# Experts of layers 0 and 1: 96 rows as three thirds in four column tiles

## The chip, the core and the metric

The kernel runs on one core of a Trainium2 chip, as one program. The metric is its device time in microseconds: 3403.63 us is the median of three runs of the kernel before (3401.73 to 3408.33). Everything is fp32. Five engines matter: TensorE (PE) multiplies, with its weight loads shown apart as PEld; VectorE (DVE), ScalarE (ACT) and GpSimd (POOL) work on tiles; SyncE (SP) issues most transfers, which 16 DMA engines carry out. ACT and POOL issue transfers too, each on a queue of its own: SP's is q1, ACT's q10, POOL's q0.

## The reference

The whole computes two transformer layers on 512 tokens of width 1024, then a third block. The part at hand is the mixture of experts at the end of each of the first two layers:

```
scores = sigmoid(x @ router_w)                      # 512 tokens x 16 experts
idx    = the two best experts of the best group;  w = their scores, made to sum to 1
rows of x are sorted by expert and padded to blocks
hb = silu(xb @ w_gate[e]) * (xb @ w_up[e])          # 1024 -> 512, twice
y  = hb @ w_down[e]                                 # 512 -> 1024
out[token] += y[row] * w
```

Each expert has three matrices of 2 MB: gate and up [1024, 512], down [512, 1024].

## The kernel before, in words

A layer's experts run in two stages, each behind a barrier of all engines: `route`, then `moe_experts`.

**Routing.** DVE works out for each token its two slots among blocks of 96 rows and, for each block, its expert (`blk_e`). POOL scatters the rows of `x` to a DRAM buffer `slots` by indirect DMA. Block 0 does not take this way: DVE builds a one-hot matrix `oneh` [token, 96], and PE multiplies (L1206) with `x` as the stationary side (128 columns of it at a time) and `oneh` as the moving side (96 columns), which gives block 0 with its features on partitions; ACT copies it from PSUM to `xg0` (L1214).

**Experts.** The trace holds 16 blocks a layer, handled in 8 pairs, each pair with two sets of buffers, r = 0 and 1. The loop's body on PE (L1468 on) is: gate and up of r = 0, of r = 1, then down of r = 0, of r = 1. A block of 96 rows is cut in a main part of 64 rows and a tail of 32:

- `gate_up` (L1436): the stationary side is 64 columns of `xg`, so the array is two column tiles of 64; gate's product goes to PSUM partitions 0 to 63, up's to 64 to 127, 512 columns each.
- `gate_up_tail` (L1446): 32 columns of `xg`, four column tiles of 32, each with 256 moving columns: two quarters for gate, two for up.
- `down` (L1458, L1464): the same cut, 64 rows in two tiles of 512 columns, 32 rows in four tiles of 256.

ACT takes a sigmoid of gate and copies up to partitions 0 to 63 (L1539, L1540, L1544, L1545), since DVE multiplies partition by partition; DVE multiplies twice (L1503, L1505, L1512, L1514) and turns the hidden rows for `down` in 32x32 blocks, one instruction for each 32 partitions (L1509 eight times, L1517 four). ACT copies the results out (L1551, L1552), and POOL stores them in six transfers a block (L1585, L1587); SP does so for the last two blocks (L1420, L1422).

**What sets the order.** Each engine runs its own loop; semaphores tie them. SP (`load_pair`) reloads a set's gate and up when the set's last gate/up matmul is done (`tail_ready`), and its down when its last down matmul is done (`down_ready`); the six loads of a pair stand in one queue in the order gate0, up0, gate1, up1, down0, down1. ACT loads the 96 rows of a coming block from `slots` (L1556, one transfer of 96 partitions by 4 KB), and DVE turns them into `xg` with twelve instructions (`turn_x`, L1497). On DVE the order is `gated(i, 0)`, `turn_x` of the next pair's r = 0, `gated(i, 1)`, `turn_x` of r = 1. `w_ready`, `xg_ready`, `hT_main`, `hT_tail` and `y_copied` are what PE waits for.

Around it: `ExpertWeights` loads four (layer 0) or five (layer 1) of the first six matrices in the stage before and the rest during `route`; `expert_sum` gathers the results after it.

Of the kernel before, what the change touches and what calls it, by code (L numbers as in the profile page):

```python
# [51 lines left out]
MOE_ROWS, MOE_BLOCKS = 96, 26  # L52
SLOT_ROWS = -(-MOE_ROWS * MOE_BLOCKS // 128) * 128
# [1104 lines left out]
def route(nc, name, x, escore, router_b, sbr, idx, strict, ones, iota, mo, xg0, slots_dram, put):  # L1158
# [5 lines left out]
    with stage(nc, name) as st:  # L1164
# [6 lines left out]
        cm, first_ps = st.ps("cm"), [st.ps(f"first{h}") for h in range(2)]  # L1171
# [16 lines left out]
        with nc.Block() as block:  # L1188
# [6 lines left out]
            @block.tensor  # L1195
            def _(pe):
                pe.wait_ge(m_ready, 1)
                nc.tensor.matmul(cm[:, 0:NT * E], strict[:], flat(both[:]), start=True, stop=False)
                nc.tensor.matmul(cm[:, 0:NT * E], ones[:], flat(acc[:, 0:NT, :]), start=False, stop=True)
                nc.tensor.matmul(cm[:, NT * E:(NT + 1) * E], ones[:], acc[:, NT, :], start=True, stop=True).then_inc(cum_ready, 1)  # L1200
                pe.wait_ge(oneh_ready, 1)
                for h in range(2):
                    for c in range(4):
                        for t in range(NT):
                            k = 4 * h + c
                            mm = nc.tensor.matmul(first_ps[h][:, c * MOE_ROWS:(c + 1) * MOE_ROWS], x[:, t, k * P:(k + 1) * P],  # L1206
                                                  oneh[:, t, :], start=(t == 0), stop=(t == NT - 1))
                    mm.then_inc(first_ready, 1)

            @block.scalar  # L1210
            def _(act):
                for h in range(2):
                    act.wait_ge(first_ready, h + 1)
                    nc.scalar.activation(xg0[:, 4 * h:4 * h + 4, :].rearrange("p c s -> p (c s)"),  # L1214
                                         first_ps[h][:, 0:4 * MOE_ROWS], ACT.Copy)
# [11 lines left out]
            def _(dve):  # L1227
# [126 lines left out]
                V.tensor_scalar(blk_e[:, B:B + 1], nbl[:], float(E // 2 - 1), None, ALU.add)  # L1354

def moe_load(sp, w, w_ready, weights, n, e, near=True):

    rows = weights[n][ds(e, 1)]
    src = rows.rearrange("a (p j) n -> p (a j) n", p=P) if near else rows.rearrange("a (k p) n -> p (a k) n", p=P)  # L1360
    sp.dma_start(w[n][:], src).then_inc(w_ready[n], 16)

def moe_experts(nc, name, sbr, xg0, slots_dram, weights, y_dram, w, w_ready, put):
# [4 lines left out]

    blk_e = sbr[4]  # L1370
    KF = D_EXP // P
    MB, MAIN, TAIL = MOE_ROWS, 64, 32
    QD = 32
    lo, hi = slice(0, MAIN), slice(MAIN, P)
    last = MOE_BLOCKS // 2 - 1
    with stage(nc, name) as st:
        xs = [st.sb(f"xs{r}", [MB, D]) for r in range(2)]
        xs_ready = [st.sem(f"xs_ready{r}") for r in range(2)]
        xg = [xg0, st.sb("xg1", [P, KD, MB])]
        sig, up, hid = ([st.sb(f"{n}{r}", [MAIN, D_EXP]) for r in range(2)] for n in ("sig", "up", "hid"))  # L1380
        tsig, tup, thid = ([st.sb(f"{n}{r}", [MAIN, D_EXP // 2]) for r in range(2)] for n in ("tsig", "tup", "thid"))
        hT = [st.sb(f"hT{r}", [P, KF, MB]) for r in range(2)]
        yb = [st.sb(f"y{r}", [P, 512]) for r in range(2)]
        ytb = [st.sb(f"yt{r}", [P, 256]) for r in range(2)]
        gu_ps = [st.ps(f"gu_ps{r}") for r in range(2)]
        tgu_ps = [st.ps(f"tgu_ps{r}", (P, 256)) for r in range(2)]
        y_ps, ty_ps = [st.ps(f"y_ps{r}") for r in range(2)], [st.ps(f"ty_ps{r}", (P, 256)) for r in range(2)]
        xg_ready = st.sem("xg_ready")
        main_ready, tail_ready = st.sem("main_ready"), st.sem("tail_ready")
        act_main, act_tail = st.sem("act_main"), st.sem("act_tail")  # L1390
        hid_main, hid_tail = st.sem("hid_main"), st.sem("hid_tail")
        hT_main, hT_tail = st.sem("hT_main"), st.sem("hT_tail")
# [6 lines left out]
        with nc.Block() as block:  # L1399

            @block.sync
            def _(sp):
                def load_pair(i):

                    e = [sp.value_load(blk_e[0:1, ds(2 * i + 2 + r, 1)], min_val=0, max_val=N_EXP - 1) for r in range(2)]
                    for r in range(2):
                        sp.wait_ge(tail_ready, 2 * i + r + 3)
                        moe_load(sp, w[r], w_ready[r], weights, 0, e[r])
                        moe_load(sp, w[r], w_ready[r], weights, 1, e[r])
                    for r in range(2):  # L1410
                        sp.wait_ge(down_ready, 2 * i + r + 3)
# [4 lines left out]
                for r in range(2):  # L1416
                    b = 2 * n1 + r
                    sp.wait_ge(y_copied, b + 3)
                    for h, part in enumerate((lo, hi)):
                        sp.dma_start(y_dram[ds(b * MB, MAIN), h * 512:(h + 1) * 512], yb[r][part, :]).then_inc(last_out, 16)  # L1420
                    for q in range(4):
                        sp.dma_start(y_dram[ds(b * MB + MAIN, TAIL), q * 256:(q + 1) * 256],  # L1422
                                     ytb[r][q * TAIL:(q + 1) * TAIL, :]).then_inc(last_out, 16)
                sp.wait_ge(last_out, 16 * 12)

            @block.tensor
            def _(pe):
                def gate_up(i, r):
                    b = 2 * i + r
                    pe.wait_ge(xg_ready, b + 1)  # L1430
                    for n in range(2):
                        pe.wait_ge(w_ready[r][n], 16 * i + 16)
                    pe.wait_ge(hid_main, b + 1)
                    for k in range(KD):
                        for n, part in enumerate((lo, hi)):
                            mm = nc.tensor.matmul(gu_ps[r][part, :], xg[r][:, k, 0:MAIN],  # L1436
                                                  w[r][n][:, k * D_EXP:(k + 1) * D_EXP], start=(k == 0), stop=(k == KD - 1))
                    mm.then_inc(main_ready, 1)

                def gate_up_tail(i, r):  # L1440
                    b = 2 * i + r
                    pe.wait_ge(hid_tail, b + 1)
                    for k in range(KD):
                        for q in range(4):
                            n, c0 = q // 2, k * D_EXP + q % 2 * 256
                            mm = nc.tensor.matmul(tgu_ps[r][q * TAIL:(q + 1) * TAIL, :], xg[r][:, k, MAIN:MB],  # L1446
                                                  w[r][n][:, c0:c0 + 256], start=(k == 0), stop=(k == KD - 1))
                    mm.then_inc(tail_ready, 1)

                def down(i, r):  # L1450
                    b = 2 * i + r
                    pe.wait_ge(hT_main, b + 1)
                    pe.wait_ge(w_ready[r][2], 16 * i + 16)
                    pe.wait_ge(y_copied, b + 1)
                    for f in range(KF):
                        for h, part in enumerate((lo, hi)):
                            c0 = f * D + h * 512
                            nc.tensor.matmul(y_ps[r][part, :], hT[r][:, f, 0:MAIN], w[r][2][:, c0:c0 + 512],  # L1458
                                             start=(f == 0), stop=(f == KF - 1))
                    pe.wait_ge(hT_tail, b + 1)  # L1460
                    for f in range(KF):
                        for q in range(4):
                            c0 = f * D + q * 256
                            mm = nc.tensor.matmul(ty_ps[r][q * TAIL:(q + 1) * TAIL, :], hT[r][:, f, MAIN:MB],  # L1464
                                                  w[r][2][:, c0:c0 + 256], start=(f == 0), stop=(f == KF - 1))
                    mm.then_inc(down_ready, 1)
# [2279 lines left out]
```

## Time and profile before

| | us |
|---|---|
| runs of the kernel before | 3401.73, 3403.63, 3408.33 |
| span of the profiled execution | 3408.2 |
| expert stage of layer 0 (first matmul to the next stage's first work) | 405.3 to 689.8 |
| expert stage of layer 1 | 1101.7 to 1385.2 |
| PE busy, DVE busy, ACT busy | 3050.8, 1764.9, 633.8 |

The page gives no time of the profiled execution apart from its span; the span is 4.6 us above the median of the runs and 0.1 us below the slowest. The two expert stages take 568 us of it, a sixth. In the page's 40 slices (85 us each) they are slices 5 to 8 and 13 to 16. A busy share is no measure of a bound: in these stages PE and the DMA engines are both busy nearly all the time, and only the waits and the landing times tell them apart. A matmul of fp32 is two instructions in the trace, each with its own weight load.

### The profile page before, as it was taken

Reading aid. Unit: us, or ns where it says so; the run is one execution under the profiler, and the core shown is the slowest. Engines: PE = TensorE matmul, PEld = TensorE weight load, DVE = VectorE, ACT = ScalarE, POOL = GpSimd, SP = SyncE. Lnnn points to the kernel's source line nnn. Section 1 sums busy time; section 2 is a strip of 40 time slices with the busy share of each in tenths; the row PEclk is TensorE's granted clock in tenths of the full one; section 3 lists DMA queues with packets and bytes.
Section 4 is the critical chain, followed back from the end, with each engine's and each line's share of the span. In section 5 each row is a group of like instructions: output and inputs, shape, how many; then the busy total and the mean of one; then the engine's idle time right before and its main releaser. Section 6 shows DMA issues by size and latency. Waiting matters only on the chain. (4 is left out here: it accounts for less than half of the span.)

```text
span 3408.2 us, 40873 instructions
## 1 busy us (share of the span) xinstructions
PE 3050.8 (90%) x15195; PEld 1424.4 (42%) x15195; DVE 1764.9 (52%) x3808; ACT 633.8 (19%) x1348; POOL 348.5 (10%) x439
## 2 busy tenths in 40 slices
PE   7888799989987999799999999898699988898887
PEld 5445433334554333454444444665432332333232
DVE  6523488732343888339999910564333242424334
ACT  1134112122321111200100110453110100101011
POOL 0113111110222111010000000123100000000000
PEclk9989799989987999799999999999799999999998
DMA  7965399840042999343335245863399999999996
GB/s 263 251 216 218 133 396 394 349 132 31 13 173 96 349 400 404 133 160 120 110 121 149 97 162 175 300 215 152 158 384 428 429 428 429 428 429 429 428 428 291
DMA packets 188225, 886.19 MB, mean 260 GB/s; under 512 B 32120, under 2 KB 71936, under 8 KB 151760
## 3 DMA queue, kind: packets, MB, share of 16 engines
q1 hardware_dynamic: 156464, 794.98, 59.4%
q0 software_dynamic: 28288, 77.91, 6.5%
q10 hardware_dynamic: 3360, 11.80, 1.1%
q8 instruction: 71, 1.16, 0.1%
q14 instruction: 42, 0.34, 0.0%
HBM read 803.59 MB, written 80.99 MB: 260 GB/s over the span
## 5 line engine op out<-in xcount | busy, mean ns | idle before, releaser
L3384 PE MATMUL ec_gu<-ec_ring,ec_xg 128*64 128x512 f32 x2032 | 484.2, 622 | 92.7 <-DVE xT L3465 56.7
L245 PE MATMUL proj_ps<-xT,proj_w 128*128 128x512 f32 x992 | 430.7, 596 | 0.0
L245 PE MATMUL proj_ps<-proj_w,xT 128*128 128x512 f32 (+2 forms) x896 | 358.3, 562 | 6.6 <-DMA proj_w<-in_w_in 4.1
L3384 PEld LDWEIGHTS ec_gu<-ec_ring,ec_xg 128*64 128x64 f32 x2032 | 151.9, 143 | 412.6 <-issue 317.9
L245 PEld LDWEIGHTS proj_ps<-xT,proj_w 128*128 128x128 f32 x992 | 189.4, 191 | 237.5 <-issue 237.0
L245 PEld LDWEIGHTS proj_ps<-proj_w,xT 128*128 128x128 f32 x896 | 171.3, 192 | 191.6 <-issue 157.3
L1497 DVE STREAM_TRANSPOSE moe_xg<-moe_xs 32x256 f32<-32x256 f32 x360 | 229.1, 637 | 38.9 <-DMA moe_xs<-slots 33.5
L1436 PE MATMUL moe_gu_ps<-moe_w,moe_xg 128*64 128x512 f32 x1024 | 231.8, 606 | 10.7 <-DVEq L1486 4.8
L3404 PE MATMUL ec_yp<-ec_ring,ec_hT 128*64 128x512 f32 x1024 | 225.8, 597 | 9.5 <-issue 6.6
L274 ACT ACTIVATE proj_o<-proj_ps 128x512 f32<-128x512 f32 (+1 forms) x120 | 70.9, 590 | 611.6 <-PE proj_ps L245 611.6
L3545 ACT ACTIVATE xT<-ec_gu 64x512 f32<-64x512 f32 x64 | 37.8, 591 | 757.3 <-PE ec_gu L3384 756.1
L2546 DVE SCALAR_TENSOR_TENSOR band_big<-proj_hit,proj_row,band_big 128x516 f32<-128x516 f32 x256 | 173.5, 749 | 2.4
L2546 DVE SCALAR_TENSOR_TENSOR band_acc<-proj_hit,proj_row,band_acc 128x512 f32<-128x512 f32 x256 | 172.5, 746 | 2.4
L3478 DVE STREAM_TRANSPOSE ec_hT<-xT 32x256 f32<-32x256 f32 x256 | 160.9, 628 | 5.5
L3465 DVE TENSOR_TENSOR xT<-xT,ec_gu 64x512 f32<-64x512 f32 x64 | 41.6, 676 | 225.4 <-ACT xT L3546 224.9
L3459 DVE TENSOR_TENSOR x<-x,ec_x 128x512 f32<-128x512 f32 x58 | 39.9, 688 | 224.5 <-PE ec_x L3364 224.4
L1458 PE MATMUL moe_y_ps<-moe_w,moe_hT 128*64 128x512 f32 x512 | 120.3, 613 | 27.2 <-DVE moe_hT L1509 27.2
L1436 PEld LDWEIGHTS moe_gu_ps<-moe_w,moe_xg 128*64 128x64 f32 x1024 | 73.2, 139 | 153.8 <-issue 153.8
L3404 PEld LDWEIGHTS ec_yp<-ec_ring,ec_hT 128*64 128x64 f32 x1024 | 72.2, 138 | 156.1 <-issue 147.0
L1446 PE MATMUL moe_tgu_ps<-moe_w,moe_xg 128*32 128x256 f32 x2048 | 117.1, 380 | 0.0
L722 PE MATMUL mix_o<-out_w,xT 128*128 128x512 f32 x256 | 112.7, 600 | 3.2 <-PEq L89 3.2
L1509 DVE STREAM_TRANSPOSE moe_hT<-moe_hid 32x128 f32<-32x128 f32 x256 | 103.1, 403 | 6.0
(527 smaller groups left out, 3626.4 us busy)
## 6 DMA issues: line engine op xcount, KB each, us to landing
ec_ring<-in_w_up SPq DMA_DIRECT2D x64, 2048.0 KB
ec_ring<-in_w_down SPq DMA_DIRECT2D x64, 2048.0 KB
ec_ring<-in_w_gate SPq DMA_DIRECT2D x63, 2048.0 KB
moe_w<-in_exp_w_gate SPq DMA_DIRECT2D x32, 2048.0 KB, 13.0
moe_w<-in_exp_w_up SPq DMA_DIRECT2D x32, 2048.0 KB, 17.0
moe_w<-in_exp_w_down SPq DMA_DIRECT2D x32, 2048.0 KB, 19.9
proj_w<-in_w_in SPq DMA_DIRECT2D x22, 2048.0 KB, 10.9
proj_w<-in_w_ada SPq DMA_DIRECT2D x16, 1536.0 KB
```

The lines of the kernel that those rows point to most:

```text
L245: mm = nc.tensor.matmul(bank[0:jb["op"], 0:jb["ow"]], lhs, rhs, start=(k == 0), stop=(k == nk - 1))
L274: e = nc.scalar.activation(row, bank, jb["func"], scale=jb["scale"])
L722: mm = nc.tensor.matmul(o_ps[t % 2][q][:], xT[:, k, t * P:(t + 1) * P], w[q][:, k, :], start=(k == 0), stop=(k == KD - 1))
L1436: mm = nc.tensor.matmul(gu_ps[r][part, :], xg[r][:, k, 0:MAIN], w[r][n][:, k * D_EXP:(k + 1) * D_EXP], start=(k == 0), stop=(k == KD - 1))
L1446: mm = nc.tensor.matmul(tgu_ps[r][q * TAIL:(q + 1) * TAIL, :], xg[r][:, k, MAIN:MB], w[r][n][:, c0:c0 + 256], start=(k == 0), stop=(k == K ...
L1458: nc.tensor.matmul(y_ps[r][part, :], hT[r][:, f, 0:MAIN], w[r][2][:, c0:c0 + 512], start=(f == 0), stop=(f == KF - 1))
L1497: e = V.transpose(xg[r][fq, :, tb], near(xs[r][tb, :], KD)[:, :, fq])
L1509: e = V.transpose(hT[r][fq, :, tb], near(hid[r][tb, :], KF)[:, :, fq])
L2546: V.scalar_tensor_tensor(acc[:, h, 0:wd], self.hit[r][:, 0:wd], self.row[r][:, h:h + 1], acc[:, h, 0:wd], ALU.mult, ALU.add)
L3384: mm = nc.tensor.matmul(gu_ps[n][half, :], xg[:, k, c0:c0 + CAP], w[m][:, j * D_FF + n * 512:j * D_FF + (n + 1) * 512], start=(k == 0), st ...
L3404: mm = nc.tensor.matmul(y_ps[half, :], hT[:, f * CAP:(f + 1) * CAP], w[:, j * D + hh * 512:j * D + (hh + 1) * 512], start=(f == 0), stop=( ...
L3478: e = V.transpose(cols.rearrange("p (d j s) -> p d j s", j=4, s=CAP)[:, :, :, tb * QD:(tb + 1) * QD], rows.rearrange("p (d q j) -> p d j q ...
```

## The change

All 96 rows are handled alike, as three thirds of 32 rows, each in four column tiles:

- `gate_up`: a third's four tiles have 256 moving columns each, 128 of gate and the same 128 of up side by side. For this gate and up lie in one SBUF tensor `[P, 2, KD * D_EXP]`. A product's gate and up columns then stand on the same partitions, so ACT makes one sigmoid of a third and DVE reads up straight from PSUM.
- `down`: a third's four tiles have 256 columns each.
- `turn_x` and the turning of the hidden rows are one instruction of 128 partitions for a third. For this `xs` holds quarter c of the features on partitions 32c to 32c+31, and its load is four transfers of 32 partitions by three runs of 1 KB.
- PSUM has three banks for gate/up and three for down, one for each third, which both sets use.
- Results are stored in four transfers a block instead of six, 32 partitions by three runs of 1 KB.
- Routing: `oneh` is the stationary side (32 columns) and `x` the moving side (256 columns); ACT copies three thirds to `first_sb`, and DVE turns them.
- All expert matrices have the near layout (a partition's rows adjacent in DRAM, 16 KB); gate and up of set 0 had the other before, in their first load. The early loads are gate0, up0, gate1, up1 (and down0 in layer 1).

```diff
@@ route
-                for h in range(2):
-                    for c in range(4):
-                        for t in range(NT):
-                            k = 4 * h + c
-                            mm = nc.tensor.matmul(first_ps[h][:, c * MOE_ROWS:(c + 1) * MOE_ROWS], x[:, t, k * P:(k + 1) * P],
-                                                  oneh[:, t, :], start=(t == 0), stop=(t == NT - 1))
+                for th in range(THIRDS):
+                    for t in range(NT):
+                        for c in range(4):
+                            mm = nc.tensor.matmul(first_ps[th][QD * c:QD * c + QD, :], oneh[:, t, th * QD:(th + 1) * QD],
+                                                  x[:, t, c * 256:(c + 1) * 256], start=(t == 0), stop=(t == NT - 1))
                     mm.then_inc(first_ready, 1)
...
+                for th in range(THIRDS):
+                    dve.wait_ge(first_copied, th + 1)
+                    V.transpose(xg0[:, th], first_sb[:, th, :].rearrange("p (q j) -> p j q", j=KD))
@@ moe_experts
+    rows_of = lambda dram, b, c: dram[ds(b * MB, MB), c * 256:(c + 1) * 256].rearrange("(t p) n -> p t n", p=QD)
...
+                    for th in range(TH):
+                        pe.wait_ge(xg_ready, TH * b + th + 1)
+                        pe.wait_ge(hid_done, TH * b + th + 1)
+                        for k in range(KD):
+                            for c, part in enumerate(quarter):
+                                c0 = k * D_EXP + c * P
+                                mm = nc.tensor.matmul(gu_ps[th][part, :], xg[r][:, th, k, :], w[r][0][:, :, c0:c0 + P],
+                                                      start=(k == 0), stop=(k == KD - 1))
+                        mm.then_inc(gu_ready, 1)
...
+                    for th in range(TH):
+                        pe.wait_ge(hT_ready, TH * b + th + 1)
+                        pe.wait_ge(y_copied, TH * b + th + 1)
+                        for f in range(KF):
+                            for c, part in enumerate(quarter):
+                                c0 = f * D + c * 256
+                                mm = nc.tensor.matmul(y_ps[th][part, :], hT[r][:, th, f, :], w[r][1][:, c0:c0 + 256],
+                                                      start=(f == 0), stop=(f == KF - 1))
+                        mm.then_inc(down_ready, 1)
...
-                    for fq in quads:
-                        for tb in quads[:MB // QD]:
-                            e = V.transpose(xg[r][fq, :, tb], near(xs[r][tb, :], KD)[:, :, fq])
+                    for th in range(TH):
+                        V.transpose(xg[r][:, th], near(xs[r][:, th, :], KD)).then_inc(xg_ready, 1)
...
+                    for th in range(TH):
+                        dve.wait_ge(act_done, TH * b + th + 1)
+                        V.tensor_mul(sig[r][:, th, :], sig[r][:, th, :], gu_ps[th][:, 0:P])
+                        V.drain()
+                        V.tensor_mul(hid[r][:, th, :], sig[r][:, th, :], gu_ps[th][:, P:2 * P]).then_inc(hid_done, 1)
+                        V.drain()
+                        V.transpose(hT[r][:, th], near(hid[r][:, th, :], KF)).then_inc(hT_ready, 1)
...
-                    act.dma_start(xs[r][:], slots_dram[ds(b * MB, MB), :]).then_inc(xs_ready[r], 16)
+                    for c, part in enumerate(quarter):
+                        act.dma_start(xs[r][part], rows_of(slots_dram, b, c)).then_inc(xs_ready[r], 16)
...
-                    for h, part in enumerate((lo, hi)):
-                        pool.dma_start(y_dram[ds(b * MB, MAIN), h * 512:(h + 1) * 512], yb[r][part, :]).then_inc(stored, 16)
-                    for q in range(4):
-                        pool.dma_start(y_dram[ds(b * MB + MAIN, TAIL), q * 256:(q + 1) * 256],
-                                       ytb[r][q * TAIL:(q + 1) * TAIL, :]).then_inc(stored, 16)
+                    for c, part in enumerate(quarter):
+                        pool.dma_start(rows_of(y_dram, b, c), yb[r][part]).then_inc(stored, 16)
```

On PE, the body of the expert loop before (names: `moe_gu_ps` and `moe_tgu_ps` are gate/up of main and tail, `moe_y_ps` and `moe_ty_ps` down of main and tail; 64x512 is 64 stationary columns by 512 moving ones):

```order
L1436 MATMUL moe_gu_ps<-moe_w,moe_xg 64x512 x16
L1446 MATMUL moe_tgu_ps<-moe_w,moe_xg 32x256 x32
L1430 REGISTER_ALU
L1436 MATMUL moe_gu_ps<-moe_w,moe_xg 64x512 x16
L1446 MATMUL moe_tgu_ps<-moe_w,moe_xg 32x256 x32
L1458 MATMUL moe_y_ps<-moe_w,moe_hT 64x512 x8
L1464 MATMUL moe_ty_ps<-moe_w,moe_hT 32x256 x16
L1458 MATMUL moe_y_ps<-moe_w,moe_hT 64x512 x8
L1464 MATMUL moe_ty_ps<-moe_w,moe_hT 32x256 x16
```

and after, from its start:

```order
L1433 MATMUL moe_gu_ps<-moe_w,moe_xg 32x256 x32
L1428 REGISTER_ALU
L1433 MATMUL moe_gu_ps<-moe_w,moe_xg 32x256 x32
L1428 REGISTER_ALU
L1433 MATMUL moe_gu_ps<-moe_w,moe_xg 32x256 x32
L1428 ISA
L1433 MATMUL moe_gu_ps<-moe_w,moe_xg 32x256 x32
L1428 REGISTER_ALU
L1433 MATMUL moe_gu_ps<-moe_w,moe_xg 32x256 x32
L1428 REGISTER_ALU
L1433 MATMUL moe_gu_ps<-moe_w,moe_xg 32x256 x32
L1446 MATMUL moe_y_ps<-moe_w,moe_hT 32x256 x96
```

Nothing changes place between the blocks; eight groups of two shapes a pair became twelve of one shape.

On ACT, the head of the loop's body before (the load of a coming block's rows, then the first block's work):

```order
L1556 DMA moe_xs<-slots 96x1024
L1539 ACT_TABLE_LOAD
L1539 ACTIVATE moe_sig<-moe_gu_ps 64x512
L1540 ACTIVATE moe_up<-moe_gu_ps 64x512
```

and after:

```order
L1517 DMA moe_xs<-slots 32x3x256
L1517 ISA
L1517 DMA moe_xs<-slots 32x3x256
L1517 ISA
L1517 DMA moe_xs<-slots 32x3x256
L1517 ISA
L1517 DMA moe_xs<-slots 32x3x256
L1505 ISA
L1506 ACT_TABLE_LOAD
L1506 ACTIVATE moe_sig<-moe_gu_ps 128x128
L1505 REGISTER_ALU
L1506 ACTIVATE moe_sig<-moe_gu_ps 128x128
```

The load stands where it stood, as four transfers of 1 KB runs instead of one of 4 KB rows.

## Rows read from the trace of the kernel before

**Rows 1.** Stretch: start:end, length, PE, PEld, DVE, ACT, POOL, clock, DMA share, GB/s.
```profile
440.00:480.00 40.00, 38.10 (x338) 14.54 (x336) 33.44 (x63) 7.79 (x15) 6.09 (x12) 0.99 1.00 393
```

**Rows 2.** Waits of TensorE, expert stage of layer 0 (two rows), then layer 1.
```profile
PE moe_y_ps L1458 <- DVE moe_hT L1509: 13.2, 7, 2.5
PE moe_gu_ps L1436 <- DMA moe_w<-in_exp_w_up: 1.5, 2, 0.8
...
PE moe_y_ps L1458 <- DVE moe_hT L1509: 14.0, 7, 2.4
```

**Rows 3.** Timeline, one pair: start us, duration us, engine, line, tiles, [idle before].
```profile
478.31 7.09 PE L1436 MATMUL moe_gu_ps<-moe_w,moe_xg 128*64 128x512 f32 x32
485.33 3.66 PE L1446 MATMUL moe_tgu_ps<-moe_w,moe_xg 128*32 128x256 f32 x64
506.95 3.65 PE L1458 MATMUL moe_y_ps<-moe_w,moe_hT 128*64 128x512 f32 x16 [1.90 <-DVE moe_hT L1509]
512.40 2.80 PE L1436 MATMUL moe_gu_ps<-moe_w,moe_xg 128*64 128x512 f32 x12
```

**Rows 4.** Weight loads (last number: us to landing) issued near 465, 636, 1322 us.
```profile
moe_w<-in_exp_w_gate SPq DMA_DIRECT2D x1, 2048.0 KB, 9.1
...
moe_w<-in_exp_w_gate SPq DMA_DIRECT2D x1, 2048.0 KB, 18.2
...
moe_w<-in_exp_w_up SPq DMA_DIRECT2D x1, 2048.0 KB, 22.0
```

**Rows 5.** DMA rate at 501:509, 478:483, 484:489; of the last, queue q10 (`moe_xs`).
```profile
DMA packets 224, 3.41 MB, mean 426 GB/s; under 512 B 16, under 2 KB 16, under 8 KB 16
...
DMA packets 265, 2.10 MB, mean 419 GB/s; under 512 B 78, under 2 KB 78, under 8 KB 150
...
DMA packets 215, 1.61 MB, mean 322 GB/s; under 512 B 42, under 2 KB 42, under 8 KB 139
...
q10 hardware_dynamic: 88, 0.33, 20.6%
```

**Rows 6.** DMA rate at 11:15 us, where rows of about 1 KB move.
```profile
DMA packets 1427, 1.43 MB, mean 357 GB/s; under 512 B 40, under 2 KB 1424, under 8 KB 1427
```

**Rows 7.** Groups: tiles xcount, busy us, mean ns of one; last, a timeline row.
```profile
L1497 DVE STREAM_TRANSPOSE moe_xg<-moe_xs 32x256 f32<-32x256 f32 x360 | 229.1, 637 | 38.9 <-DMA moe_xs<-slots 33.5
L1446 PE MATMUL moe_tgu_ps<-moe_w,moe_xg 128*32 128x256 f32 x2048 | 117.1, 380 | 0.0
...
60.74 1.50 PE L233 MATMUL proj_ps<-proj_w,condT 128*1 128x96 f32 x64
```

**Rows 8.** Timeline, routing to the first reload of a weight buffer, layer 0.
```profile
390.68 10.27 PE L1206 MATMUL route_first<-route_oneh,x 128*128 128x96 f32 x64 [4.97 <-DVE route_oneh L1340]
400.98 0.49 ACT L1214 ACTIVATE moe_xg<-route_first 128x384 f32<-128x384 f32 x1 [3.08 <-PE route_first L1206]
405.31 9.60 PE L1436 MATMUL moe_gu_ps<-moe_w,moe_xg 128*64 128x512 f32 x32 [4.37 <-issue]
418.71 0.36 SPq L1361 DMA_DIRECT2D moe_w<-in_exp_w_gate  x1
```

**Rows 9.** Stretches of the routing matmuls, columns as in rows 1.
```profile
390.00:397.00 7.00, 6.33 (x31) 6.33 (x31) 2.01 (x8) 0.00 (x0) 5.17 (x7) 0.52 0.83 329
397.00:401.00 4.00, 3.94 (x36) 3.78 (x34) 0.00 (x0) 0.51 (x2) 1.78 (x2) 1.00 0.98 382
```

**Rows 10.** Timeline, end of the expert stage of layer 0; last row: layer 1.
```profile
660.27 7.09 PE L1436 MATMUL moe_gu_ps<-moe_w,moe_xg 128*64 128x512 f32 x32 [0.84 <-DMA moe_w<-in_exp_w_up]
679.91 1.93 PE L1464 MATMUL moe_ty_ps<-moe_w,moe_hT 128*32 128x256 f32 x32
684.40 2.35 SPq L1422 DMA_DIRECT2D slots<-moe_yt  x4
689.79 0.17 DVE L1076 CAST exp_idx<-posA 128x4 uint32<-128x4 f32 x1 [13.59 <-PEq L1642]
...
1355.78 7.09 PE L1436 MATMUL moe_gu_ps<-moe_w,moe_xg 128*64 128x512 f32 x32
```

More of the change, by code:

```diff
@@ L52 @@
 MOE_ROWS, MOE_BLOCKS = 96, 26
+QD = 32
+THIRDS = MOE_ROWS // QD
 SLOT_ROWS = -(-MOE_ROWS * MOE_BLOCKS // 128) * 128
@@ L1211, in _ @@
             def _(act):
[L1212 to L1215, printed above, removed]
+                for th in range(THIRDS):
+                    act.wait_ge(first_ready, th + 1)
+                    nc.scalar.activation(first_sb[:, th, :], first_ps[th][:], ACT.Copy).then_inc(first_copied, 1)
             @block.gpsimd
@@ L1354, in _ @@
                 V.tensor_scalar(blk_e[:, B:B + 1], nbl[:], float(E // 2 - 1), None, ALU.add)
[L1357 to L1361, printed above, removed]
+                for th in range(THIRDS):
+                    dve.wait_ge(first_copied, th + 1)
+                    V.transpose(xg0[:, th], first_sb[:, th, :].rearrange("p (q j) -> p j q", j=KD))
@@ L1608, in __init__ @@
         self.weights = [a[n][i] for n in ("exp_w_gate", "exp_w_up", "exp_w_down")]
-        self.w = [[None] * 3, [None] * 3]
+        self.w = [[None] * 2, [None] * 2]
         self.w_ready = [[nc.alloc_semaphore(f"moe{i}_w_ready{n}{r}") for n in range(3)] for r in range(2)]
-        self.place(self.ORDER[:early], "right")
+        self.place(self.BUFFERS[:early], "right")
     def place(self, which, side):
-        for r, n in which:
-            self.w[r][n] = self.hold.enter_context(self.nc.sbuf_tensor(f"moe{self.i}_w{n}{r}", [P, KD * D_EXP], F32, side=side))
+        for r, down in which:
+            shape = [P, KD * D_EXP] if down else [P, 2, KD * D_EXP]
+            self.w[r][down] = self.hold.enter_context(self.nc.sbuf_tensor(f"moe{self.i}_w{down}{r}", shape, F32, side=side))
     def load(self, sp, which):
-        for r, n in which:
-            moe_load(sp, self.w[r], self.w_ready[r], self.weights, n, r, near=(r == 1 or n == 2))
+        for r, down in which:
+            for n in ((2,) if down else (0, 1)):
+                moe_load(sp, self.w[r], self.w_ready[r], self.weights, n, r)
     def begin(self, sp):
-        self.load(sp, self.ORDER[:self.early])
+        self.load(sp, self.BUFFERS[:self.early])
     def rest(self, sp):
-        self.load(sp, self.ORDER[self.early:])
+        self.load(sp, self.BUFFERS[self.early:])
     def close(self):
```

161 lines of the change are left out of this document (48 added, 113 removed).

## The prediction

> **What bounds the kernel now.** I read the stretches first, then the waits of TensorE, then one pair in the timeline, then the landings of the weight loads, then DMA rates. The stretches show PE busy 38.1 of 40 us at a clock of 0.99 and the DMA engines at a share of 1.00 [rows 1]; neither number says which of them holds the other up. The waits do: in layer 0 PE waits 13.2 us in 7 pieces for the turned hidden rows before `down` of r = 1, and 1.5 us in 2 for an up matrix; in layer 1 it waits 14.0 us for the former [rows 2]. By that PE seems the bound. The timeline gives its pair: 478.31 to 512.40, 34.1 us, 1.9 of them that wait [rows 3].
>
> The landings say otherwise. The gate load of r = 1 issued near 465 us lands after 9.1 us, the one near 636 us, five pairs later, after 18.2 us [rows 4]. The queue falls behind by (18.2 - 9.1) / 5 = 1.8 us a pair, so the DMA needs 34.1 + 1.8 = 35.9 us for a pair. It has a head start (the first pair's six matrices are there when the stage begins), and spends it: in layer 0 the last pair's gate/up of r = 1 starts at 660.27, after a wait of 0.84 us for its up matrix [rows 10]. So layer 0 ends on the chain of loads. In layer 1 the up load of r = 0 issued near 1322.4 lands 22.0 us later, at 1344.4 [rows 4]; gate and up of r = 1 take two more times 2.10 MB / 426 GB/s = 4.9 us, so the last up is there at 1354.3. PE starts on it at 1355.78 [rows 10]. A landing is seen some 0.7 us later, so PE was at most 0.8 us behind the loads: both layers stand on the DMA chain, nearly to the microsecond, and what PE and DVE save inside a pair has nowhere to go.
>
> What the 35.9 us are: a pair moves 6 x 2.10 MB of weights, 0.79 MB of `xs` and 0.79 MB of results, 14.16 MB. At the 426 GB/s of a stretch with weights alone that is 33.2 us. Stores beside them cost nothing (419 GB/s), but while an `xs` load runs the whole falls to 322 GB/s [rows 5]: q10 moved 0.33 of its 0.39 MB in those 5 us, so a load takes 6 us and costs 6 x (1 - 322/426) = 1.5 us, twice a pair. 33.2 + 2.9 = 36.1 us, beside 35.9 from the landings.
>
> **The change, part by part.**
>
> *PE.* Three gate/up thirds and three down thirds a block are 192 + 96 matmul instructions, 576 a pair, in fours that run beside each other. A tail group of 64 is busy 3.66 us [rows 3] and its last one lasts 0.38 [rows 7]: 3.28 us for 15 steps of four, 0.217 us with the start of the four. So a pair takes 144 x 0.217 = 31.2 us, against 32.2 at work before. That PE is fed fast enough shows in 64 matmuls in 1.50 us elsewhere [rows 7]. The wait for hidden rows goes: DVE needs 24 turns of 0.637 us a pair for `xg` alone now [rows 7] and six afterwards. One of 128 partitions is not in the trace; if it took four times as long, DVE would do what it does now, which PE bears. PE's pair is 31.2 us, 2.9 less. Inside the loop this counts for nothing, for the next loads are what PE waits for; the waits grow to 36.3 - 31.2 = 5.1 us a pair. Before the first matmul of the stage PE sat idle 4.37 us and its first group took 9.60 us instead of 7.09 [rows 8, 3]; 2.5 us of that sort a pair still fit into 5.1.
>
> *The chain of loads.* It starts when gate/up of block 0 ends: 418.71, with the first reload [rows 8]. The last up lands after six pairs and four of six loads, 6.7 periods.
>
> (a) Start. The routing product takes 10.27 us [rows 8], 6.3 of them at a clock of about 0.5 and the rest at 1.0 [rows 9]. Afterwards it is 96 instructions, 24 fours: 14.5 in those 6.3 us at 0.43 us each and 9.5 at 0.217, 8.4 us in all. Behind it came an ACT copy of 0.49 us, now one of some 0.4 and a turn of 0.64 that was not there: 10.27 + 0.5 becomes 8.4 + 0.2 + 0.4 + 0.7, 1.1 us less. If the clock rose later it would be nothing; if the turn is dear, 1 us more. I take -1.1 a layer.
>
> (b) Period. The `xs` load is 384 runs of 1 KB instead of 96 of 4 KB. Rows of that size alone move at 357 GB/s [rows 6] against 426: 0.79 MB take 2.2 us instead of 1.85, +0.36 us a pair. The slowing of everything else during `xs`, 2.7 to 2.9 us a pair, is the open price. If it goes by bytes (a run holds up another engine's write as long as it lasts), it stays. If it goes by the number of runs, it is four times that. If it came from 96 partitions being cut unevenly over 16 engines, it goes. I take bytes, since 88 packets of q10 took 20.6% of 16 engines over 5 us [rows 5], 0.19 us each, hardly over the 0.15 us that 4 KB need at 426 GB/s: what was lost was lost in the big weight rows, in step with the share of time that `xs` had. Period 36.3 us. Bounds: 33.2 + 0.4 = 33.6, and 36.3 + 3 x 2.7 = 44.4. Times 6.7: +2.4 a layer.
>
> (c) After the last up: a gate/up and two downs, 96 fours, 20.8 us and 0.2 for the last to end, against 660.27 to 681.84 [rows 10]: -0.6.
>
> (d) Last results. From PE's end at 681.84 to the end of SP's sixth issue at 686.75 are 4.9 us [rows 10]; four issues at the 0.59 us that its row gives, after one copy of 0.4 us, make 3.1: -1.8. The gather behind it waits for them.
>
> Layer 0: -1.1 + 2.4 - 0.6 - 1.8 = -1.1. Layer 1: the same, but the 0.8 us that PE was behind is no longer in it: -1.9. Together -3.0 us on a span of 3408.2, and so on the median of 3403.63, from which the span differs by 0.13%: **3400.6 us**. Of the other edits: ACT's three more issues of `xs` a block (some 0.35 us each), the sigmoids by thirds and the copies lie beside PE, ACT being busy 7.8 of 40 us [rows 1]; the early loads and the near layout lie in stages that do not wait for them. What is queued behind the new wait: `turn_x` of r = 0 now stands longer on DVE, because q10's rows take turns with weight rows. 24 runs an engine, each behind a 16 KB row of 0.62 us, are 16 to 18 us. They start at the pair's start, and behind them waits `gated(i, 1)`, whose result PE wants 28 us in. It fits; two such loads fill 32 to 36 of 36.3 us, so there is little room.
>
> A rule speaks against this load. The Trainium skill, SBUF — State Buffer, section "Door 1: The DMA port swizzle", says that partitions 0 to 31 reach no more than 8 of the 16 ports by which transfers enter SBUF, as 0 to 63 do. The mechanism without the page: in the 484 to 489 us stretch the writes of `xs` held up the weight rows, and packing them on fewer places would raise the price; that is the second rival.
>
> **Rivals.**
>
> 1. *The slowing goes* . If the uneven cut of 96 partitions made it, 32 at a time divides evenly. For it: stores of 64 and 32 partitions do no harm [rows 5]; against: these read SBUF. With half or all of it gone the period is 34.9 to 33.6: (1.4 to 2.7) x 13.4 = 19 to 36 us off: 3381, at most 3364. I give 33%.
>
> 2. *The slowing grows* (slower). Place: q10 in the loop. With 1 KB runs `xs` is in flight nearly all the time, and the low rate holds for longer. For it: 322 GB/s whenever q10 is at work, and the rule above. Against: q10's own packets were hardly longer. From a period of 37.0 us (0.7 over mine) it decides; at 38.3 it costs 2.0 x 13.4 = 27: 3427. With the full price by runs, 44.4, it would be 3509. I give 28%.
>
> 3. *PE's gain shows.* Were the loads not the bound, 7 pairs x 2.9 us x 2 = 41 us would go, and the 8 of (a), (c), (d) and layer 1's 0.8: 3355. The landings exclude it, since 33.2 us is the least the bytes need. 1%.
>
> 4. *Quartered matmuls are slower in a row of 576*, through the moving side in two pieces of 128 columns, which the trace does not have: over 0.252 us a four PE is the bound again; at 0.26 it is 37.4 us a pair: 3415. 3%.
>
> **How the numbers follow.** My case (period 36.0 to 37.0) has 35%. A difference below 0.2%, 6.8 us, cannot be told from no change here: faster means below 3396.8, a period under 36.0; slower above 3410.4, a period over 37.0. Faster 0.34, same 0.35, slower 0.31. Range: cases of both signs hold most of the chance; my own case alone spans 3396 to 3411. For 8 in 10 it reaches down to all but the last of rival 1, 3370, and up to a period of 39, 3438.
>
> **What would show it.** Landings: with the period right, the gate load of r = 1 lands later by its lag behind PE, and PE shows waits of some 5 us a pair before L1433, on gate or up. Wait on `hT` gone: step PE right. DMA rate while q10 is at work: near 400 GB/s with q10 spread over most of the pair means by bytes; above 415, rival 1; below 380, rival 2. First reload near 417.6: (a). From PE's end to the gather's first work 6 us instead of 8: (d). The prediction is wrong if PE waits for `xg` or if the pairs last under 35 or over 38 us.

## The result and the profile after

The changed kernel takes 3417.31 us in the median of 8 runs (3413.22 to 3421.01), against 3407.17 us for the kernel before in as many beside it: ratio 1.0031, 95% interval [1.0022, 1.0040]. It is slower by 10 us where 3 us of gain were forecast. The traces have spans of 3417.5 and 3408.2 us.

The stretch of [rows 1] and the waits of TensorE of [rows 2], after (the first three waits are layer 0, the rest layer 1; they are given as total us, count, longest):

```profile
440.00:480.00 40.00, 39.87 (x744) 25.81 (x736) 9.14 (x24) 7.58 (x17) 5.62 (x11) 1.00 1.01 404
```
```profile
DVE moe_xg L1474 <- DMA moe_xs<-slots: 157.7, 13, 14.5
PE moe_y_ps L1446 <- issue: 13.3, 5, 3.3
PE moe_gu_ps L1433 <- DVE moe_hid L1482: 7.7, 5, 2.5
...
DVE moe_xg L1474 <- DMA moe_xs<-slots: 181.1, 14, 13.9
PE moe_y_ps L1446 <- issue: 13.9, 5, 3.4
PE moe_gu_ps L1433 <- DVE moe_hid L1482: 7.3, 5, 2.2
```

The first stretch looks better than before: PE busy throughout, VectorE at 9 us instead of 33. The new row is VectorE's wait for the rows of x, up to 14.5 us each; before it was 16.5 us in one piece in all of layer 0. One pair in the timeline, the fourth of layer 0 ([rows 3] have the third of before), shows what hangs on it (PE, ScalarE's queue and VectorE, in order of time):

```profile
512.50 10.55 PE L1433 MATMUL moe_gu_ps<-moe_w,moe_xg 128*32 128x256 f32 x192
513.22 1.78 ACTq L1517 DMA_DIRECT2D moe_xs<-slots  x4
521.14 1.73 DVE L1474 STREAM_TRANSPOSE moe_xg<-moe_xs 128x256 f32<-128x256 f32 x3 [13.49 <-DMA moe_xs<-slots]
523.26 1.82 ACTq L1517 DMA_DIRECT2D moe_xs<-slots  x4
523.55 10.57 PE L1433 MATMUL moe_gu_ps<-moe_w,moe_xg 128*32 128x256 f32 x192 [0.51 <-DVE moe_hid L1482]
533.91 5.39 PE L1446 MATMUL moe_y_ps<-moe_w,moe_hT 128*32 128x256 f32 x96
539.60 1.67 DVE L1474 STREAM_TRANSPOSE moe_xg<-moe_xs 128x256 f32<-128x256 f32 x3 [13.59 <-DMA moe_xs<-slots]
542.39 7.07 PE L1446 MATMUL moe_y_ps<-moe_w,moe_hT 128*32 128x256 f32 x96 [3.09 <-issue]
549.26 10.57 PE L1433 MATMUL moe_gu_ps<-moe_w,moe_xg 128*32 128x256 f32 x192
557.88 1.72 DVE L1474 STREAM_TRANSPOSE moe_xg<-moe_xs 128x256 f32<-128x256 f32 x3 [13.51 <-DMA moe_xs<-slots]
```

The rows asked for at 513.22 are turned at 539.60, those of 523.26 at 557.88: 26 and 35 us later. Before, the rows asked for at 523.29 had their last packet in at 532.4. Between 466 and 632 us the turns follow each other at 18.3 to 18.7 us, so a pair lasts two of them: 549.26 - 512.50 = 36.8 us. `gated(i, 1)` stands behind `turn_x` on VectorE, so `down` of r = 1 starts 3.1 us late, and then takes 7.07 us instead of 5.39, since TensorE's clock has fallen to 0.76 of full speed in the mean of that stretch (last number but two):

```profile
542.00:549.00 7.00, 6.61 (x92) 4.56 (x96) 2.04 (x7) 0.77 (x2) 0.79 (x2) 0.76 1.02 406
```

**Where the time went.** The expert stage of a layer, from its first gate/up product to the next stage's first `exp_t` product, lasts 292.1 and 291.5 us before, 294.0 and 295.0 after. Repeated traces give sums of 583.6, 582.8, 583.7 before and 589.1, 588.8 after: 5.6 us are lost here, in means. The other 4 to 5 us arise in code that the change does not touch (last part of the experiments).

Layer 0 in pieces, before by [rows 8, 10], after by these:

```profile
402.65 0.96 POOL L1223 DMA_INDIRECT slots<-x,moe_idx  x1 [0.30 <-issue]
403.32 0.63 DVE L1358 STREAM_TRANSPOSE moe_xg<-route_first_sb 128x256 f32<-128x256 f32 x1 [1.06 <-ACT route_first_sb L1216]
409.80 16.43 PE L1433 MATMUL moe_gu_ps<-moe_w,moe_xg 128*32 128x256 f32 x268 [6.97 <-issue]
422.35 0.36 SPq L1365 DMA_DIRECT2D moe_w<-in_exp_w_gate  x1
...
659.21 20.93 PE L1433 MATMUL moe_gu_ps<-moe_w,moe_xg 128*32 128x256 f32 x384
679.93 10.57 PE L1446 MATMUL moe_y_ps<-moe_w,moe_hT 128*32 128x256 f32 x192
685.96 6.99 SPq L1418 DMA_DIRECT2D slots<-moe_y  x8
696.22 0.17 DVE L1078 CAST exp_idx<-posA 128x4 uint32<-128x4 f32 x1 [14.54 <-PEq L1601]
```

| piece | before | after | difference |
|---|---|---|---|
| first gate/up to first reload | 13.40 | 12.55 | -0.85 |
| first reload to last gate/up (r = 1) | 241.56 | 247.30 | +5.75 |
| last gate/up to PE's end | 21.57 | 20.85 | -0.7 |
| PE's end to the next stage's work | 7.95 | 5.7 | -2.2 |

(The last r = 1 gate/up starts at the middle of the 20.93 us row, 669.65.) Their sum is 2.0 us. In layer 1 the first piece is -0.2 (13.36 to 13.15 us), the second +6.6 (240.7 to 247.3), the last two together -2.9.

### The profile page after: what moved, and what is told of

Read it like the earlier page. It is cut to its first block and busy times, and to the rows that moved or that the text cites. A ratio compares the mean times of both kernels' runs of the same rounds, so it can differ in the third digit from the quotient of the medians.

```text
span 3417.5 us, 50265 instructions
## 1 busy us (share of the span) xinstructions
PE 3042.0 (89%) x19867; PEld 1563.5 (46%) x19867; DVE 1454.7 (43%) x3320; ACT 607.5 (18%) x1350; POOL 323.9 (9%) x383
## 5 line engine op out<-in xcount | busy, mean ns | idle before, releaser
L1433 PE MATMUL moe_gu_ps<-moe_w,moe_xg 128*32 128x256 f32 x6144 | 346.0, 386 | 30.5 <-issue 15.5
L1433 PEld LDWEIGHTS moe_gu_ps<-moe_w,moe_xg 128*32 128x32 f32 x6144 | 234.1, 112 | 139.6 <-issue 23.8
L1446 PE MATMUL moe_y_ps<-moe_w,moe_hT 128*32 128x256 f32 x3072 | 179.8, 392 | 27.5 <-issue 27.2
L1474 DVE STREAM_TRANSPOSE moe_xg<-moe_xs 128x256 f32<-128x256 f32 x90 | 51.0, 618 | 352.7 <-DMA moe_xs<-slots 338.8
L1446 PEld LDWEIGHTS moe_y_ps<-moe_w,moe_hT 128*32 128x32 f32 x3072 | 119.2, 113 | 84.8 <-issue 39.3
L1544 POOL DMA_DIRECT2D slots<-moe_y x112 | 61.3, 548 | 466.7 <-ACT moe_y L1513 303.2
```

What stands on the lines that cost most here:

```text
L1433: mm = nc.tensor.matmul(gu_ps[th][part, :], xg[r][:, th, k, :], w[r][0][:, :, c0:c0 + P], start=(k == 0), stop=(k == KD - 1))
L1446: mm = nc.tensor.matmul(y_ps[th][part, :], hT[r][:, th, f, :], w[r][1][:, c0:c0 + 256], start=(f == 0), stop=(f == KF - 1))
L1474: V.transpose(xg[r][:, th], near(xs[r][:, th, :], KD)).then_inc(xg_ready, 1)
L1544: pool.dma_start(rows_of(y_dram, b, c), yb[r][part]).then_inc(stored, 16)
```

## The experiments

All are edits of the changed kernel unless told otherwise. "Stages" are the two expert stages of a kernel's trace.

| | a block's rows of x | turns | stages, us | median, us | ratio to before |
|---|---|---|---|---|---|
| before | 96 x 4 KB, one transfer | 12 | 292.1, 291.5 | 3407.2 | |
| after | 384 x 1 KB, 32 partitions | 3 | 294.0, 295.0 | 3417.3 | 1.0031 |
| e1 | the same; VectorE's order | 3 | 293.2, 294.5 | 3415.0 | 1.0027 [1.0017, 1.0037] |
| e2 | 96 x 4 KB | 12 | 284.8, 288.2 | 3398.5 | 0.9981 [0.9971, 0.9990] |
| e3 | 384 x 1 KB, 96 partitions | 12 | 290.1, 290.5 | 3406.1 | 1.0001 [0.9992, 1.0010] |
| e4, e8 | 192 x 2 KB, 96 partitions | 12 | 284.1, 281.2 (e8) | 3391.6, 3390.9 | 0.9946 [0.9932, 0.9959] (e8) |
| e5 | 96 x 4 KB, 32 partitions | 12 | 291.7, 291.9 | 3409.8 | 1.0011 [1.0001, 1.0021] |
| e6 | before, new routing | 12 | 292.7, 291.6 | 3405.7 | 1.0000 [0.9991, 1.0009] |
| e7 | 384 x 1 KB, 128 partitions | 3 | 370.1 (layer 0) | 3563.0 | 1.0458 [1.0444, 1.0473] |
| e9 | none in the loop | 12 | 265.0, 264.7 | 3359.6 | 0.9861 [0.9846, 0.9876] |
| e10 | 384 x 1 KB, 32 partitions | 12 | 309.5, 308.0 | 3445.1 | 1.0110 [1.0092, 1.0128] |
| e11 | e8, and e1's order | 12 | 279.9, 281.5 | 3388.5 | 0.9950 [0.9934, 0.9966] |
| e12 | before, none in the loop | 12 | 306.8, 308.3 | 3436.3 | 1.0085 [1.0067, 1.0103] |

**e1.**
```
-                    turn_x(2 * i + 2, 0, i + 1)
                     gated(i, 1)
+                    turn_x(2 * i + 2, 0, i + 1)
```

> The changed kernel with one edit: on VectorE gated(i, 1) stands ahead of the turn of x for the next pair's first block. Theory A (head of line): the loss inside the expert stages comes from turn_x waiting up to 14 us for its rows of x while gated(i, 1) stands behind it on VectorE; it delays hT of the second block (3 us a pair on TensorE) and the release of gu_ps (1.5 us a pair). Then TensorE's waits on hT and hid go, the last first-block gate/up of layer 0 starts when its up weight lands (8 us earlier than now), the second when the last up lands (663.7 us in the changed trace), and each layer ends 4 to 5 us sooner: 3407 to 3410 us, about the kernel before. Theory B (chain of loads): the stage is bound by the weight stream with its period of 35.5 us, TensorE's waits only fill its slack, and the order on VectorE is worth under 1 us a layer: 3416 to 3418 us.

Near theory B's time (3415.0 us, 1 us under its range), but not for its reason. The wait on hT went, and PE's wait for a free PSUM bank grew from 7.7 to 17.2 us in layer 0: now `gated` of the next pair stood behind both late turns. The wait moved because its source had stayed.

**e2.**
```
-    xs = [P, TH, 256], four transfers;  V.transpose(xg[r][:, th], near(xs[r][:, th, :], KD))
+    xs = [MB, D];  act.dma_start(xs[r][:], slots_dram[ds(b * MB, MB), :])
+    for fq in quarter: V.transpose(xg[r][fq, th], near(xs[r][tb, :], KD)[:, :, fq])
```

> The changed kernel with the rows of x loaded as before the change: one transfer of 96 runs of 4 KB a block in place of four transfers of 96 runs of 1 KB, and so twelve turns a block (7.8 us on VectorE) in place of three (1.7 us). Theory A (late rows because of their 384 short packets, which take turns with the weight packets): a load lands about 5 us after its issue instead of 25 to 34 us, VectorE's waits for it go from 13 us to under 2, and the time falls to 3408 to 3412 us in spite of 6 us more of turns a block. Theory B (chain of loads): same as the changed kernel, 3416 to 3418 us; if the twelve turns delay gated(i, 1) as much as the late rows did, 3416 to 3420 with the wait gone and the turn in its place.

The rows' load alone is worth 16 us of stages: 3398.5 us, under both kernels and 10 us under theory A's range, with 6 us more of turns a block. The last packet of a load is in 9 us after its issue, and between 420 and 650 us VectorE no longer waits for rows at all. The queues between 470 and 610 us (packets, MB, share of 16 engines), before, after and e2:

```profile
q1 hardware_dynamic: 3370, 49.19, 87.9%
q10 hardware_dynamic: 896, 3.15, 7.0%
```
```profile
q1 hardware_dynamic: 3418, 49.71, 89.0%
q10 hardware_dynamic: 3417, 3.01, 6.5%
```
```profile
q1 hardware_dynamic: 3462, 50.43, 88.3%
q10 hardware_dynamic: 896, 3.15, 6.5%
```

In the changed kernel 49.71 MB in pieces of 16 KB are 3034 weight packets, and 3.01 MB in pieces of 1 KB are 2940 rows of x: one for one. Since a pair needs 768 of each, this count alone does not show how the engines choose. e8 below does: its pair needs 768 weight packets and 384 pieces of rows, and yet in 511 to 519 us, while a load runs, 2.67 MB of weights (163 pieces of 16 KB) and 0.34 MB of rows (166 of 2 KB) move:

```profile
q1 hardware_dynamic: 189, 2.67, 86.2%
q10 hardware_dynamic: 183, 0.34, 11.8%
```

So q10 takes no more of the engines than before, it takes turns. A weight packet lasts 0.890 x 16 x 140 / 3034 = 0.657 us and a short one 0.05, so 24 of each an engine need 17.0 us, and the results' stores on q0 (5.9% of the engines) about 1 more; 140 us held 2940/384 = 7.66 loads, 18.3 us each, the spacing of the turns. That both loads of a pair fill its 36.6 us was within what the prediction called "little room".

**e3, e4, e5: count against width.** Over e2, four column pieces of 1 KB; two of 2 KB; three transfers of 32 whole rows.

> As e2_rows_4k (x in 96 partitions, twelve turns a block), but a block's rows come as four transfers, each one 1 KB column piece of all 96 rows: 384 packets of 1 KB over 96 partitions. Theory P (packets take turns): each of the 16 engines sends one short packet for each 16 KB weight packet (47 and 656 ns in the changed trace), so 24 short packets an engine need 24 x 0.70 = 17 us, and the second load of a pair stands behind the first: waits for the rows as in the changed kernel (13 us each), and with twelve turns on top 3417 to 3426 us. Theory W (width: a transfer to 32 partitions only is what is slow): rows land within 10 us of their issue and the time is that of e2_rows_4k, 3397 to 3400 us.

> As e2_rows_4k, with two transfers a block, each half of the columns of all 96 rows: 192 packets of 2 KB. Theory P: 12 x (0.66 + 0.09) = 9 us of packets and some 3 us ahead of the first, landing 12 to 13 us after issue, early enough for the turns: 3398 to 3403 us. Theory W: as e2_rows_4k, 9 us.

> As e2_rows_4k, with three transfers a block, each 32 whole rows to 32 partitions: 96 packets of 4 KB. Theory P: the count of packets is the same, so the rows land 9 to 10 us after issue and the time stays at 3397 to 3400 us. Theory W: landing later than 15 us, VectorE waits for it, 3405 us or more.

Both theories have a part. By count alone, with all 96 partitions (e3 over e2), the stages get 7.6 us longer and VectorE waits for rows again (59.8 us in 11 waits in 420 to 650 us); 2 KB still land in time, and e4 and e8 are the fastest of these, with stages 5 to 8 us under e2's, a gain over e2 that no theory had. By width alone, with 4 KB (e5 over e2), they get 10.6 us longer, against theory P, but not by theory W's late rows: VectorE waits for them 3.3 us in all. The queue rows of e5, as above:

```profile
q1 hardware_dynamic: 3308, 48.17, 87.7%
q10 hardware_dynamic: 1152, 3.15, 6.9%
```

A weight packet lasts 0.877 x 2240 / 2940 = 0.668 us, against 0.883 x 2240 / 3078 = 0.643 in e2: beside the narrow load the stream is 4% slower. This is the second rival's mechanism, and the Trainium skill's rule (SBUF — State Buffer, "Door 1: The DMA port swizzle") points the same way, though e5 shows only the loss, not the ports. In the changed kernel the price shows against e3, the same 1 KB pieces over 96 partitions: 0.657 us, 0.653 in its second trace, against 0.869 x 2240 / 3059 = 0.636. Against the kernel before (0.879 x 2240 / 3002 = 0.656) it does not show, and why that one, with e2's load, lies 2% over e2 was not looked for; so the size of the price is known less well than its sign.

**e7.**
```
-    four transfers: xs[r][part] <- rows_of(slots_dram, b, c)
+    three transfers: xs[r][:, th, :] <- slots_dram[ds(b * MB + th * QD, QD), :].rearrange("p (c n) -> c p n", c=4)
```

> The changed kernel with a block's rows of x in three transfers, a third each, spread over all 128 partitions (128 runs of 1 KB), in place of four, each to 32 partitions. The 384 packets of 1 KB and the three turns stay. Theory P (count of packets alone): 17.5 us a load, TensorE's pair stays at two loads, 35 to 37 us: 3412 to 3417 us. Theory P+W (the count, and 32-partition transfers on top, as e3 against the changed kernel and e5 against e2 suggest): some loads take 11 to 12 us, as in e3, and with three turns in place of twelve 3402 to 3408 us.

Both theories fail, by 150 us. ScalarE stood at its own issue, for 18.9 to 31.1 us four times in layer 0, with the sigmoids behind it, and the queue tells why:

```profile
499.55 30.49 ACTq L1518 DMA_DIRECT2D moe_xs<-slots  x3
...
q10 hardware_dynamic: 2790, 2.77, 5.9%
```

2.77 MB are 2705 packets, so 85 of the 2790 are markers (short packets that close a transfer, one on each engine that took part), for 21 transfers: 4 each. In the changed kernel 3417 - 2940 = 477 markers go with 30.6 transfers, 16 each. So this shape ran on four engines: its outermost dimension is 4. The Trainium skill (DMA: Bandwidth & Descriptors, "Why a DMA increments its semaphore by 16 and not by 1") gives that rule, the largest number up to 16 that divides the slowest dimension on both sides, and the trace agrees. Width was thus not all that e7 varied.

**e6.** 

> The kernel before with the routing part of the change alone (one-hot as stationary side, copies and three turns, first weights in the same order as all others). Theory A (the scatter sets the end): the product is 2.7 us shorter, but the first gate/up of the experts comes 5.8 us after GpSimd's last scatter transfer is issued, in both traces, so the stage from the routing's first product (384 us) to the first gate/up stays at 21.1 us within 0.3, and the time at that of before within 0.1%. Theory B (the product was on the path): 1 us sooner a layer, 3403 us. On the first projections: should the 5 us that the changed kernel loses before 204 us come with the new routing's program, they are there in this run too; otherwise it stands as the kernel before.

Theory A. In the kernel before, after and e6 the first gate/up comes 6 us after GpSimd's last scatter is done issuing; the shorter product has nothing to give. The first attention is reached 1.2 us later than in the first trace of before.

**e8, e11: the version that beats both.** 

> e4_rows_2k_wide unchanged, in more rounds, as the candidate that beats both kernels: 3390 to 3396 us, 0.3 to 0.5% under the kernel before. If its first result was luck of four runs, it comes out with e2_rows_4k at 3397 to 3400 us.

> e8_rows_2k_again with the order of e1 on VectorE (gated(i, 1) ahead of the turn of x for the next pair). In e8 VectorE waits 12 us in all for rows in layer 0 and TensorE about 5 for the turn, so the order has little to give: 3388 to 3392 us, within 0.1% of e8's 3390.9. Should the turn of 7.2 us ahead of gated(i, 1) delay the reloads, 3385 or less.

e8 repeats e4: 0.54% under the kernel before. With rows in time the order on VectorE brings 0.1% at most (3388.5; the intervals overlap).

**e9, e12: without the rows.** 

> e8 with the rows' loads inside the loop left out: the turns take the rows loaded once before it, so all pairs but the first compute on stale rows. What the weight stream is without them. By bytes a pair's rows are 2 x 12 packets an engine x 0.09 = 2.2 us of the period of 35.0: the period falls to 33 us, TensorE's own 31.9 stays under it, and the time falls by 10 to 15 us a layer, to 3365 to 3380 us. If short packets take turns at no cost to the weights, or the stage is bound by TensorE, less than 5 us a layer.

> The kernel before with the rows' loads inside the loop left out (stale rows after the first pair), as e9 does for the changed form. Theory A (TensorE's gain is real and hidden under the weight stream): the loop is bound by TensorE at the pair of 34.1 us instead of 31.2 in e9, so the two stages last 2 x 6.5 x 2.9 = 38 us longer than e9's 528.4, less what the stream gives: 560 to 568 us of stages, 3382 to 3390 us. Theory B (the matmuls of the changed form bring nothing of their own): the stream sets both, and it comes out within 10 us of e9's 3359.6 us.

e9 came out under its range of 3365 to 3380 us. Its loop is bound by TensorE; pairs start 31.1 us apart:

```profile
505.47 20.91 PE L1433 MATMUL moe_gu_ps<-moe_w,moe_xg 128*32 128x256 f32 x384
526.19 10.55 PE L1446 MATMUL moe_y_ps<-moe_w,moe_hT 128*32 128x256 f32 x192
536.55 20.91 PE L1433 MATMUL moe_gu_ps<-moe_w,moe_xg 128*32 128x256 f32 x384
```

With rows the up matrices of r = 0 land 35.0 us apart in e8, so loading them costs at least 3.9 us a pair: 2.2 by their bytes, the rest in slower weight packets (0.647 instead of 0.614 us, 48 of them: 1.6).

e12 went against both theories: slower than with the rows, by 28 us. Nine of its twelve pairs in the loop last 37.0 us, three 35.3. With no transfer to issue, ScalarE's table load (1.28 us) slid behind the wait for the first product; everything on VectorE came that much later, and the wait of [rows 3] grew from 1.90 to 3.15 us:

```profile
510.28 5.35 PE L1458 MATMUL moe_y_ps<-moe_w,moe_hT 128*64 128x512 f32 x16 [3.15 <-DVE moe_hT L1509]
```

The same 16 matmuls took 3.65 us after 1.90 us of waiting [rows 3]. So 1.25 us of wait and 1.70 us of lower clock are the 2.9 us of the pair. In the pairs of 35.3 us the wait is the same and the clock stays: at 584.36, after 3.14 us, the 16 matmuls take 3.65 us. As a measure of the stream e12 is void; its TensorE-bound pairs of 35.3 to 37.0 us, beside 34.1 in the kernel before, do show that the old form needs more than the 31.1 us of the new one.

**e10.** 

> As e2_rows_4k, a block's rows in twelve transfers, each a 1 KB column piece of 32 rows to 32 partitions: the fourth of the combinations of count and width. The two expert stages last 573.0 us together in e2 (96 packets, wide), 580.6 in e3 (384, wide), 583.6 in e5 (96, narrow) and 589 in the changed kernel (384, narrow, three turns). Theory P+W, the two prices adding: 591 us of stages, 3415 to 3420 us. Theory P, count alone, e5's loss being something else: 581 us of stages, 3405 to 3408 us. Twelve issues of 0.45 us on ScalarE stand in for four and may add up to 2 us a layer.

3445.1 us with 617 us of stages, 26 above theory P+W. Its twelve issues a block put ScalarE in the way: its waits of kind "issue" before sigmoids and table loads are 54.9 us in 420 to 650 us. It changed two things at once, so whether the prices of count and width add stays open.

**The code that was not changed.** 

> The kernel before, once more, for its trace alone. If the shift of 5.9 us that arose between 93 and 224 us (the first projections, untouched by the change) and that of 4.4 us in the scan at 880 to 942 us belong to the programs, this trace shows those stages as the first one does, within 0.5 us; if they are scatter between executions, they lie several us apart.

> The changed kernel, once more, for its trace alone: the same question for the first projections (93 to 224 us) and for the scan (886 to 952 us). Belonging to the program: both as in the first trace within 0.5 us. Scatter: several us apart. The expert stages should repeat within 1 us.

> The kernel before a third time, for its trace: the first attention's first product came at 224.0 and 222.6 us in its two traces, 225.2 in e6, and at 225.5 to 230.1 in seven traces of the changed kernel and its variants. If the first projections' time belongs to the program, 222 to 225.5 again; if it is scatter, anywhere up to 230.

The first attention starts at 224.0, 222.6 and 222.9 us in three traces of the kernel before, 225.2 in e6 and 224.7 in e12; in twelve of the changed kernel and its variants at 225.2 to 230.1, 227.5 in the mean. The two groups differ by 3.6 us, in stages with the same instructions; traces of one program lie up to 1.4 us apart, more than the 0.5 that was expected of either. In both traces of the changed kernel TensorE waits there for a load, by 3.0 and 3.1 us, which no trace of the kernel before shows, and the clock is lower (0.83 instead of 0.92 over 125 to 160 us):

```profile
PE proj_ps L247 <- DMA proj_w<-in_na_w_in: 3.0, 1, 3.0
```

Why this load comes later in these programs was not found. The scan, 880 to 942 us, costs 4.4 us more in the changed kernel, 2.4 in its second trace, 0.0 to 2.5 in the variants, and nothing in the repeats of before, e6 and e12. One place where it loses time can be read, before and after:

```profile
897.64 0.92 PE L2075 MATMUL scan_n<-mli_v,scan_wt 128*128 128x193 f32 x4 [1.41 <-DVE scan_wt L2139]
898.40 1.88 PE L2059 MATMUL scan_s<-mli_q,mli_k 96*128 96x512 f32 x4
```
```profile
905.19 1.65 PE L2034 MATMUL scan_n<-mli_v,scan_wt 128*128 128x193 f32 x4 [2.54 <-DVE scan_wt L2098]
906.64 3.62 PE L2018 MATMUL scan_s<-mli_q,mli_k 96*128 96x512 f32 x4
```

VectorE's two small instructions ahead of it (128x4) take 1.22 and 2.22 us after, 2.16 and 0.17 before; in both traces the long one ends within 0.1 us of GpSimd's own instruction. So TensorE waits 1.1 us longer, and its matmuls take twice as long for the next 5 us. Which of them meets GpSimd differs between the two traces, though the code is the same; that this meeting is the cause was not tested.

## Why the prediction was wrong

- **PE's pair: right.** 31.2 us forecast, 31.1 in e9, 0.216 us a four (the rows of the prediction give 3.28 / 15 = 0.219, not 0.217; it changes nothing). Rival 4 did not happen, and the gain of rival 3 shows in e9, once the loads are relieved.
- **(a) Start: the mechanism wrong, the number partly right by luck.** The product took 7.6 us, under the 8.4 forecast, but the first gate/up came no sooner for it. [rows 8] show only that PE, ScalarE and the first gate/up follow each other, not that one releases the other; the constant 6 us behind GpSimd's scatters points to these (e6). The first reload came 0.85 us sooner in layer 0 and 0.2 in layer 1, but behind the start of gate/up, where no term had put it; 1.1 was forecast.
- **(b) Period of the loads: nearly right as a number.** 35.5 us between landings of r = 0's up, in the changed kernel and in the second trace of before alike, against 36.3 forecast. The DMA rate, 399 GB/s with q10 in flight all the time, is the sign that was named for this case. By the prediction's own scale a period under 36.0 meant a faster kernel; it came out slower, since the period of the loads was no longer the stage's pace.
- **(c), (d): right.** -0.7 and -2.2 us against -0.6 and -1.8 (the terms given for (d), 4 x 0.59 + 0.4, make 2.8 and not 3.1, so -2.1, which is nearer still). The 0.7 us from a landing to the start behind it, on which layer 1's 0.8 us rests, is 0.24 to 0.27 us in the waits for weights that the first trace of before holds; the sum would change by under 0.5 us.
- **"It fits": the step that failed.** The prediction worked out 16 to 18 us of turns a load and set this against the 28 us within which PE wants the result. But the loads of r = 0 and r = 1 follow each other on q10, each may be issued only when its buffer is turned, and each took 18.3 us: two make a chain of 36.6 us a pair, longer than the loads' 35.5, and rows are turned 26 to 35 us after they are asked for. TensorE no longer waited for weights but for VectorE, behind it, with the clock on top: +5.75 and +6.6 us in the second piece, where +2.4 was forecast. The prediction's own sign, PE waiting for `xg`, came true: its weight loads wait for it five times in layer 0, 10.0 us in all. e2 takes the short packets away and the stages fall by 16 us.
- **Rival 1** (33%) did not happen: with 32 partitions at a time the weight packets get longer, not shorter (e5 over e2).
- **Rival 2** had the sign, and width slows the stream (e5); the time, 3417.3 us, lies on its side of the range 3370 to 3438. But the chain of rows was in it only as "in flight nearly all the time". Its price was given to the weights, and it fell on the rows.
- Of the 10 us, 5.6 are explained by this. The rest lies in untouched stages, the first projections and the scan, with some scatter behind them; in the scan a longer wait and a lower clock can be read at one place, and the cause of both parts stays open.

## What to carry to other kernels

A transfer's price has two parts: its bytes, and the number of its packets on each engine times the length of a packet of the queue with which it takes turns. Compare the second with the time in which the data are wanted, and add up the loads that stand in one queue before comparing. If an edit makes an engine faster by cutting a load into shorter runs, try the old load with the new compute first (here e2, e8): the gain and the loss came from different halves of one change.

## What the runs showed of the hardware

- Two queues with work share the engines one packet for one packet, whatever their sizes: 163 of 16 KB to 166 of 2 KB in 8 us of e8, 3034 of 16 KB to 2940 of 1 KB in 140 us of the changed kernel.
- Beside a load to 32 partitions the weight stream's 16 KB packets lasted 0.668 us, beside the same load to 96 partitions 0.643 us.
- A load whose outermost dimension is 4 ran on 4 engines and held ScalarE at its issue for up to 31 us.
- A `STREAM_TRANSPOSE` costs the same on 32 and on 128 partitions: 0.637 us [rows 7] and 0.618 us for 256 columns.
- The length of a wait alone did not decide TensorE's clock. It stayed full after 1.90 us in the kernel before; in the trace after it stayed full after 3.14 us (579.2 to 584.5 us: 1.00) and fell after 2.28 us (597.2 to 600.2 us: 0.59).
